# One queue for the first loads, a mixed priority for the planner, and state stores on the scalar engine's queue, in an eight-core diffusion step

## The chip, the cores and the metric

The kernel runs on all eight cores of one Trainium2 chip. Each core runs the same program on its own data. The time is the device time of the slowest core in microseconds (us); lower is better. The profile is that of one execution, taken on the slowest core.

## The reference, cut to what matters

Two trunk layers of width 1024 are applied to 512 context tokens (two new requests of 256) and 1024 latent tokens per core.

```
h = rmsnorm(x) * (1 + sc) + sh                      # sc, sh, g: six slices of silu(c) @ ada_w
layer 0:  q, k, v, g, lr_f, lr_b, fin = split(h @ ev_w_in)
          o  = gated linear attention, both directions, 4 heads, scan over chunks:
               S = decay * S + k^T v ;  o = q S + masked(q k^T) v
          o  = rmsnorm(o) * silu(g) ;  fo = Re(2-D DFT(fin))
          x += g_m * (concat(o, fo) @ ev_w_out)
layer 1:  gelu / spatial gating and a gated width-3 convolution, then an output projection
both:     x += g_f * (relu(h @ ffn_w1)^2 @ ffn_w2)
out:      rmsnorm(x), and the final scan states of the context requests (fwd and bwd)
```

## The kernel before, in words

The 1536 tokens of a core lie in three chunks of 512: chunks m = 0 and 1 are latent, m = 2 is context. `xT[m]` (2 MB, float32) holds the residual, `hT[m]` the normalised bfloat16 input. Weights come in units of 1 MB in bfloat16, cast from 2 MB of float32 on the way by the GpSimd queue, into six slots (`NW = 6`). The slot of each unit is fixed by program order (`wload`), so a unit can be loaded only when the unit six places before it in its slot has been read for the last time. Two units, `qk0` and `qk1`, hold their slots for longer (`pinned`).

The program records operations in program order (`R.add`, one `seq` number each). A planner (`schedule`) then gives each engine a fixed order: step by step it takes, over all engines, the operation that can start earliest by its own cost figures, and where several can start at the same time, the one with the lowest `prio`. Before the change `prio` is `seq`. The engines then run their lists in order, with semaphore waits where one depends on another. The planner charges a switch of the scalar engine's function table 1300 ns, and it gives out the eight banks of PSUM.

In program order the work is: four units of the adaLN projection (`ada0_s0` to `ada0_s3`), each needed by two of the eight columns of the first norm; the norm of chunks 0 and 1; `evc` (the small input projections, weight `evC`: decay inputs `lrT` and Fourier input `finT`); `xcs_tile`; the norm and `evc` of chunk 2; then for head 0 `Dunit` (decays, four activations of 1024 columns) and `QK`; the values and gates `vg` of 12 token tiles by three units; `headS(h)` for the latent tokens of the four heads, with eight scan steps (`step`) in a chain and four output pairs (`opair`); `headP(h)` for the context tokens, two steps each, whose final states are stored to `ns`; the DFTs; `og_T`, the output projection `outproj`; the norm; and the FFN, in which each unit of `wf1` is used for twelve groups (four output columns times three chunks) and each of `wf2` for six.

During the attention the space of `xT` holds other tiles (`vtokS`, `sprevS`, `xcs`, `qke`), so x is loaded a second time before the output projection: chunks 0 and 1 when those tiles are free, chunk 2 after the last context head. `Rp` holds the context scan states and is used again by each head, so the first state copy of head h + 1 waits until the stores of head h have landed.

All first loads of x and the stores go through the SyncE queue (SP); all cast loads through the GpSimd queue (POOL).

Of the kernel before, what the change touches and what calls it, by code (L numbers as in the profile page):

```python
# [7 lines left out]
BF16 = mybir.dt.bfloat16  # L8
# [30 lines left out]

class Op:  # L40
    __slots__ = ("eng", "parts", "seq", "prio", "tab", "lat", "dma", "newpt", "pts",
                 "succ", "npred", "ext", "ready", "start", "fin", "key", "val", "dur")


class Rec:
# [105 lines left out]
    def schedule(self):  # L151
        ops = self.ops
# [3 lines left out]
        for o in ops:  # L156
            preds = set()
            for _, deps, _ in o.parts:
                preds |= deps
            o.npred = len(preds)  # L160
            for p in preds:
                p.succ.append(o)
        cand = {e: [] for e in self.ENGS}
        for o in ops:
            if o.npred == 0:
# [169 lines left out]
def _consts():  # L335
    c = {}
    s = np.arange(128)[:, None]
    t = np.arange(128)[None, :]
    cb = np.zeros((128, 1152), np.float32)
    cb[:, 0:128] = np.eye(128)  # L340
    cb[:, 128:256] = (s <= t) / 16.0
    cb[:, 256:384] = (s >= t) / 16.0
    cb[:, 384:512] = (s <= t)
    cb[:, 512:640] = (s >= t)
    a = np.arange(64)
    ang = 2 * np.pi * ((a[:, None] * a[None, :]) % 64) / 64.0
    for g in range(2):
        cb[g * 64:(g + 1) * 64, 640 + g * 64:640 + (g + 1) * 64] = np.cos(ang)
        cb[g * 64:(g + 1) * 64, 768 + g * 64:768 + (g + 1) * 64] = np.sin(ang)
    cb[:, 896:1024] = 1.0 / 1024  # L350
    cb[:, 1024:1152] = 1.0
    c["cb"] = cb
    mats = {}
    for L in (256, 1024):
        tt = np.arange(L, dtype=np.int64)
        ang = 2 * np.pi * ((tt[:, None] * tt[None, :]) % L).astype(np.float64) / L
        sc = 1.0 / np.sqrt(64.0 * L)
        mats[L] = ((np.cos(ang) * sc).astype(np.float32), (-np.sin(ang) * sc).astype(np.float32))
    u = [mats[1024][k][:, m * 512:(m + 1) * 512].reshape(8, 128, 512).transpose(1, 0, 2)
         for m in range(2) for k in range(2)]  # L360
    c["dft1024"] = np.ascontiguousarray(np.stack(u).reshape(4, 128, 4096))
    u = [mats[256][k].reshape(2, 128, 256).transpose(1, 0, 2) for k in range(2)]
    c["dft256"] = np.ascontiguousarray(np.stack(u, 2).reshape(128, 1024))
    return c
# [5 lines left out]
def build():  # L370
    nc = bass.Bass("TRN2", target_bir_lowering=False)

    def din(name, shape):
        return nc.dram_tensor(name, list(shape), F32, kind="ExternalInput").ap()
# [15 lines left out]
    wodo_d = din("wodo", [2, 128, 4096])  # L390
    wf1_d = din("wf1", [16, 128, 4096])
    wf2_d = din("wf2", [16, 128, 4096])
    cb_d = din("cb", [128, 1152])
    dft1024_d = din("dft1024", [4, 128, 4096])
    dft256_d = din("dft256", [128, 1024])
    y_d = dout("y", [3, 8, 128, 512])
# [2 lines left out]
    with contextlib.ExitStack() as es:  # L399
        A0 = (nc.sbuf_base + 63) // 64 * 64  # L400
        R = Rec(nc, es)
        cur = [A0]

        def at(nbytes):
            a = cur[0]
            cur[0] += (nbytes + 63) // 64 * 64
            assert cur[0] <= nc.sbuf_usable_end, cur[0]
            return a


        cb = R.sb("cb", [128, 1152], BF16, at(2304))
        identb, tri = cb[:, 0:128], [cb[:, 128:256], cb[:, 256:384]]
        mask2, cs64, onesb = cb[:, 384:640], cb[:, 640:896], cb[:, 896:1024]
        ones33 = cb[0:33, 1024:1152]
        wsT = R.sb("wsT", [128, 512], BF16, at(1024))
        w2aug = R.sb("w2aug", [64, 1024], BF16, at(2048))
        gbr = R.sb("gbr", [33, 512], BF16, at(1024))
        pp = R.sb("pp", [128, PP_N], F32, at(PP_N * 4))
        scT = R.sb("scT", [128, 8, 2], BF16, at(32))
        cst = R.sb("cst", [128, 2], F32, at(8))  # L420
        modT = [R.sb("modT%d" % l, [128, 48, 2], F32, at(384)) for l in range(2)]
        gsc = [R.sb("gsc%d" % l, [128, 2, 8, 2], F32, at(128)) for l in range(2)]
# [60 lines left out]
            R.add(q, [(lambda: h.dma_start(out=dst, in_=src), [], 1000 if q == "pool" else 100)], W=[dst],  # L483
                  dma=(key, nbytes), prio=prio)

        def store(dst, src, key, nbytes):
            R.add("sp", [(lambda: nc.sync.dma_start(out=dst, in_=src), [src], 100)], W=[], dma=(key, nbytes))


        wpos = [0]  # L490
# [13 lines left out]
        def w8(name, src, pin=None):  # L504
            return wload(name, src, 4096, pin)[:].rearrange("p (k n) -> p k n", k=8)
# [4 lines left out]
        def cload(dst, src, q):  # L510
            ksp[0] += 1
            load(q, dst, src, "dc%d" % ksp[0], nfree(dst) * 128 * 4)

        R.add("dve", [(lambda: nc.vector.memset(cst[:, 0:1], EPS), [], 70)], W=[cst[:]])
        R.add("dve", [(lambda: nc.vector.memset(cst[:, 1:2], 1.0), [], 70)], W=[cst[:]])
        cload(pp[:], pp_d, "sp")
        load("sp", xT[0][:].rearrange("p c t -> p (c t)"), x_d[0], "dx0", 2 << 20)
        act(scT[:], pp[:, PP_COND:PP_COND + 16].rearrange("p (c k) -> p c k", k=2), AF.Silu, [pp[:]], [scT[:]], tab="silu")

        def evac_mod(l, ps, c0, nch, pc0):  # L520
# [35 lines left out]
        def norm_stats(m, x):  # L556
            ps = PT(R)
            parts = []
            for c in range(8):
                sq = ring(sqr)  # L560
                act(sq[:], x[:, c, :], AF.Square, [x[:, c, :]], [sq[:]])
                R.add("pe", [(lambda sq=sq, c=c: nc.tensor.matmul(ps.f(), onesb, sq[:], start=(c == 0), stop=(c == 7)), [sq[:], onesb], 216)], W=[ps])  # L562
            r = ring(rsr)
            act(r[:], lambda: ps.f(), AF.Ln, [ps, cst[:]], [r[:]], tab="nle", bias=cst[:, 0:1])
            act(r[:], r[:], AF.Exp, [r[:]], [r[:]], tab="nle", scale=-0.5)
            return r
# [27 lines left out]

        for u in range(4):
            ada_unit("ada0_s%d" % u, wada_d[u], 0, [(u * 2, 2, 0), (8 + u * 2, 2, 2)])
            if u == 0:
                cload(cb[:], cb_d, "pool")
        norm(0, 0, 0)
        load("sp", xT[1][:].rearrange("p c t -> p (c t)"), x_d[1], "dx1", 2 << 20)  # L600
        norm(0, 0, 1)
        load("sp", xT[2][:].rearrange("p c t -> p (c t)"), x_d[2], "dx2", 2 << 20)


        xo = [a_x]
# [34 lines left out]
        vtok = lambda j: vtokS[:, j, :] if j < 8 else vtokP[:, j - 8, :]  # L640
        sprev = lambda d, j: sprevS[:, d, j, :] if j < 8 else sprevP[:, d, j - 8, :]

        cload(w2aug[:], w2aug_d, "pool")
        R.add("pool", [(lambda: nc.gpsimd.memset(lrT[32:64, :], 0.0), [], 900)], W=[lrT[:]])
        R.add("pool", [(lambda: nc.gpsimd.memset(lrT[32:33, :], 1.0), [], 900)], W=[lrT[:]])

        wc = wload("evC", wevc_d, 2304)[:].rearrange("p (k n) -> p k n", k=8)

        def evc(m):
            p = PT(R)  # L650
# [87 lines left out]
        def step(h, fw, i, Rt, d_is, seqn):  # L738
# [20 lines left out]
            for d in range(2):  # L759
# [10 lines left out]
                if last:  # L770
                    j = tl[d]
                    act(r[:], r[:], AF.Identity, [r[:], dc[:]], [r[:]], scale=dc[:, d, j:j + 1])
                    store(ns_d[d, seqn, h], r[:], "dns%d%d" % (d, seqn), 128 * 768)

        def opair(h, ja):

# [63 lines left out]
            for d in range(2):  # L840
                load("sp", Rs[h % 2][d][:], s0_d[d, h], "ds0%d%d" % (h % 2, d), 128 * 768)

        wqk = {0: w8("qk0", wev_d[0], 0)}
        wv = [w8("vg%d" % u, wev_d[2 + u]) for u in range(3)]
        wqk[1] = w8("qk1", wev_d[1], 1)
        norm(0, 0, 2)
        evc(2)
# [46 lines left out]
        ada(0, 2)  # L894
        wO = [w8("evO%d" % i, wevo_d[i]) for i in range(2)]
        for m in range(2):
            load("sp", xT[m][:].rearrange("p c t -> p (c t)"), x_d[m], "dx%d" % m, 2 << 20)

        def outproj(l, wo, src, m):
            for oc in range(8):  # L900
# [14 lines left out]
        norm(0, 1, 0)  # L915
        for j in range(8, 12):
            og_T(j)
        load("sp", xT[2][:].rearrange("p c t -> p (c t)"), x_d[2], "dx2", 2 << 20)
        outproj(0, wO, hT, 2)
        norm(0, 1, 1)  # L920
        norm(0, 1, 2)
# [253 lines left out]
```

How the kernel before makes its waits and increments, by code:

```python
    def emit(self):  # L269
# [31 lines left out]
                    if need.get(d.key, 0) < d.val:  # L301
                        need[d.key] = d.val
                items = sorted(need.items(), key=lambda kv: kv[0])
                semof = lambda key: sem[key] if key in sem else self.dsem[key]
                todo = []
                for key, val in items:
                    if know[e].get(key, 0) < val:
                        todo.append((key, val))
                        learn(e, key, val)
                for key, val in todo[:-1]:
                    H[e].wait_ge(semof(key), val)
                ins = fn()
                if todo:
                    ins._wait_ge(semof(todo[-1][0]), todo[-1][1])
# [4 lines left out]
                dcnt[key] = dcnt.get(key, 0) + 16  # L319
                ins.then_inc(self.dsem[key], 16)
                o.key, o.val = key, dcnt[key]
            else:
                cnt[e] += 1
                ins.then_inc(sem[e], 1)
                o.key, o.val = e, cnt[e]
            snap[(o.key, o.val)] = dict(know[e])
        for key, val in list(dcnt.items()):
            if know["sp"].get(key, 0) < val:
                nc.sync.wait_ge(self.dsem[key], val)
        for e in self.ENGS:
            if cnt[e] and know["sp"].get(e, 0) < cnt[e]:
                nc.sync.wait_ge(sem[e], cnt[e])
```

## Time and profile before

| what | value |
|---|---|
| time, median of 3 runs | 1254.83 us (1253.84 to 1268.19) |
| the profiled execution's own time | 1252.24 us |
| its span on the slowest core | 1250.9 us (all cores 1237.9 to 1250.9) |
| TensorE (PE) busy | 1138.3 us, 91% |
| VectorE (DVE) busy | 451.0 us, 36% |
| ScalarE (ACT) busy | 437.5 us, 35% |
| read from HBM | 171.5 MB |

The span is the time from the first to the last instruction; 1.3 us of the execution lie outside it. PE is the busiest engine by far, and the other engines matter where PE waits for them.

### The profile page before, as it was taken

To read this page: it belongs to the slowest core of one execution; us is meant where nothing else is said; L and a number is where in the kernel's file an instruction comes from. 1 tells how busy PE (TensorE), PEld (TensorE's weight loads), DVE (VectorE), ACT (ScalarE), POOL (GpSimd) and SP (SyncE) were. 2 spreads that over 40 slices of the span, in tenths; PEclk is the share of its full clock that TensorE was granted. 3 is DMA by queue.
4 is the path that set the end of the run, shared out by engine and by line. 5 is a ranking of instruction groups with operands and counts; after the bars stand their busy time and mean duration, and the time that the engine had idled before them with its cause. 6 is when DMAs were issued, how large, how long until landed. Compare 5 with 4: busy or idle time off the path is not lost.

```text
span 1250.9 us, 15212 instructions; the slowest of 8 cores (1237.9 to 1250.9 us)
## 1 busy us (share of the span) xinstructions
PE 1138.3 (91%) x6288; PEld 542.5 (43%) x6288; DVE 451.0 (36%) x883; ACT 437.5 (35%) x834; POOL 48.4 (4%) x109
## 2 busy tenths in 40 slices
PE   0599978789849999999999999999999999999995
PEld 0144455454414444444444444444444444444442
DVE  0364156676633222222222341456532222222226
ACT  1661377753644320023310383225543100332013
POOL 2000000000000000000000000000000000000000
PEclk9699989889969999999999989999999999999997
DMA  9984241569783245447535212105313131310005
GB/s 236 175 140 74 42 89 26 85 118 223 119 181 68 37 98 101 80 90 135 100 58 112 45 25 39 30 1 101 68 35 68 34 68 34 68 34 1 1 1 201
DMA packets 19344, 101.36 MB, mean 81 GB/s; under 512 B 2155, under 2 KB 5483, under 8 KB 9036
## 3 DMA queue, kind: packets, MB, share of 16 engines
q0 software_dynamic: 11312, 79.01, 35.5%
q1 hardware_dynamic: 7964, 21.39, 5.2%
q8 instruction: 49, 0.80, 0.3%
q14 instruction: 19, 0.16, 0.0%
HBM read 171.53 MB, written 7.86 MB: 143 GB/s over the span
## 4 chain that ended last, share of the span: by engine, by line
PE 81%; DMA 10%; ACT 4%; DVE 3%; issue 1%; POOL 0%; DVEq 0%; ACTq 0%; POOLq 0%
PE ps L461 79%; DMA w_ada_s_77<-wada 4%; DMA xT_73<-x 3%; DMA ns<-RP_93 2%; PE ps L1007 1%; PE ps L562 1%; DMA w_ada_3_0_129<-wada 1%; ACT sprevS L471 1%; ACT hT_68 L471 0%; ACT hT_69 L471 0%; ACT sq_59 L471 0%; ACT junk L471 0%; DVE og L799 0%; ACT t_3_101 L471 0%; ACT sq_60 L471 0%
## 5 line engine op out<-in xcount | busy, mean ns | idle before, releaser
L471 ACT ACTIVATE relu_65<-ps 128x512 bf16<-128x512 f32 x64 | 38.2, 597 | 242.0 <-PE ps L461 242.0
L471 ACT ACTIVATE relu_67<-ps 128x512 bf16<-128x512 f32 x64 | 38.2, 597 | 68.2 <-PE ps L461 68.2
L471 ACT ACTIVATE relu_66<-ps 128x512 bf16<-128x512 f32 x64 | 38.2, 597 | 67.1 <-PE ps L461 67.1
L938 DVE TENSOR_TENSOR aT_133<-relu_65 128x512 bf16<-128x512 bf16 x60 | 25.5, 426 | 79.0 <-ACT relu_65 L471 79.0
L938 DVE TENSOR_TENSOR aT_135<-relu_67 128x512 bf16<-128x512 bf16 x60 | 25.5, 426 | 78.1 <-ACT relu_67 L471 78.1
L938 DVE TENSOR_TENSOR aT_134<-relu_66 128x512 bf16<-128x512 bf16 x60 | 25.5, 426 | 75.9 <-ACT relu_66 L471 75.9
L471 ACT ACTIVATE sq_58<-xT_71 128x512 bf16<-128x512 f32 x15 | 9.4, 628 | 113.1 <-PE ps L562 87.5
L582 DVE SCALAR_TENSOR_TENSOR xT_73<-ps,modT_50,xT_73 128x512 f32<-128x512 f32 x24 | 17.4, 748 | 53.6 <-PE ps L461 41.4
L582 DVE SCALAR_TENSOR_TENSOR xT_73<-ps,modT_51,xT_73 128x512 f32<-128x512 f32 x24 | 18.0, 751 | 50.9 <-PE ps L461 50.9
L582 DVE SCALAR_TENSOR_TENSOR xT_72<-ps,modT_50,xT_72 128x512 f32<-128x512 f32 x24 | 17.9, 750 | 50.1 <-PE ps L461 46.7
L582 DVE SCALAR_TENSOR_TENSOR xT_71<-ps,modT_51,xT_71 128x512 f32<-128x512 f32 x24 | 18.0, 751 | 48.7 <-PE ps L461 48.7
L582 DVE SCALAR_TENSOR_TENSOR xT_71<-ps,modT_50,xT_71 128x512 f32<-128x512 f32 x24 | 17.7, 750 | 48.9 <-PE ps L461 47.8
L582 DVE SCALAR_TENSOR_TENSOR xT_72<-ps,modT_51,xT_72 128x512 f32<-128x512 f32 x24 | 17.7, 750 | 47.0 <-PE ps L461 47.0
L562 PE MATMUL ps<-sq_58,cb 128*128 128x512 bf16 x40 | 17.3, 434 | 11.1 <-DMA cb<-cb 7.9
L471 ACT ACTIVATE og<-ps 128x256 bf16<-128x256 f32 (+1 forms) x24 | 11.8, 491 | 43.3 <-DVE vtokS L592 24.7
L471 ACT ACTIVATE junk<-ps 128x192 bf16<-128x192 f32 x48 | 15.8, 329 | 22.0 <-PE ps L461 21.7
L562 PE MATMUL ps<-sq_59,cb 128*128 128x512 bf16 x40 | 17.7, 443 | 4.2 <-ACT sq_59 L471 3.6
L461 PE MATMUL ps<-scT,w_ada_s_74 128*128 128x2 bf16 x32 | 1.0, 166 | 22.2 <-DMA w_ada_s_74<-wada 22.2
L562 PE MATMUL ps<-sq_60,cb 128*128 128x512 bf16 x40 | 17.6, 440 | 4.0 <-ACT sq_60 L471 3.4
L471 ACT ACTIVATE sq_60<-xT_71 128x512 bf16<-128x512 f32 x10 | 6.3, 626 | 42.1 <-DVE xT_71 L582 36.0
L523 DVE TENSOR_TENSOR modT_50<-ps,pp 128x4 f32<-128x4 f32 (+1 forms) x16 | 2.2, 158 | 51.0 <-PE ps L461 51.0
L799 DVE SCALAR_TENSOR_TENSOR og<-ps,rs,og 128x192 bf16<-128x192 f32 x48 | 17.7, 410 | 6.4 <-ACT rs L471 6.1
(719 smaller groups left out, 2412.8 us busy)
## 6 DMA issues: line engine op xcount, KB each, us to landing
xT_71<-x SPq DMA_DIRECT2D x2, 2048.0 KB, 16.2
xT_72<-x SPq DMA_DIRECT2D x2, 2048.0 KB, 27.2
xT_73<-x SPq DMA_DIRECT2D x2, 2048.0 KB, 35.9
w_ada_s_74<-wada POOLq DMA_DIRECT2D x1, 1024.0 KB, 20.6
w_ada_s_75<-wada POOLq DMA_DIRECT2D x1, 1024.0 KB, 37.1
w_ada_s_76<-wada POOLq DMA_DIRECT2D x1, 1024.0 KB, 43.1
w_ada_s_77<-wada POOLq DMA_DIRECT2D x1, 1024.0 KB, 49.9
w_qk_115<-wev POOLq DMA_DIRECT2D x1, 1024.0 KB, 56.1
```

Source lines behind the costliest of these rows:

```text
L461: parts.append((lambda view=view, l=l, r=r, i=i, n=n: nc.tensor.matmul(view(), l, r, start=(i == 0), stop=(i == n - 1)), [l, r], max(27.0, ...
L471: R.add("act", [(lambda: nc.scalar.activation(out=o(), in_=i(), func=func, **kw), Rd, dur)], W=W, tab=tab)
L523: lambda: nc.vector.tensor_tensor(out=modT[l][:, c0:c0 + nch, :], in0=ps.f(pc0 * 2, (pc0 + nch) * 2).rearrange("p (c k) -> p c k", k=2), i ...
L562: R.add("pe", [(lambda sq=sq, c=c: nc.tensor.matmul(ps.f(), onesb, sq[:], start=(c == 0), stop=(c == 7)), [sq[:], onesb], 216)], W=[ps])
L582: lambda: nc.vector.scalar_tensor_tensor(out=x[:, oc, :], in0=ps.f(), scalar=modT[l][:, gch + oc, CI(m):CI(m) + 1], in1=x[:, oc, :], op0=A ...
L799: lambda o_=o_, t=t: nc.vector.scalar_tensor_tensor(out=o_, in0=ps.f(t * 192, t * 192 + 192), scalar=rs[:, k + t:k + t + 1], in1=o_, op0=A ...
L938: vop(2, [a], [rl[:]], lambda a=a, rl=rl: nc.vector.tensor_tensor(out=a, in0=rl[:], in1=rl[:], op=ALU.mult))
L1007: parts.append((lambda g=g, l_=l_, r_=r_, i=i, p=p: nc.tensor.matmul(p.f(g * 128, (g + 1) * 128), l_, r_, start=(i == 0), stop=(i == 1)), ...
```

## The change

The planner's priority becomes 30 times the sequence number minus `bl`, the longest path in the planner's nanoseconds from the operation to the end of the program (a DMA counts with its issue and a fixed latency in it, not with its transfer). The first loads of x move from the SP queue to the POOL queue, where they stand in one list with the weights; the second loads stay on SP. `w2aug`, `cb`, `evC`, `qk0` and `vg0` are recorded earlier, before or between the first norms. The matrix of 1/1024 that the norm's sums use is no longer part of `cb`; VectorE sets it by a memset. The stores of the context states go to the scalar engine's queue; the stores of y stay on SP.

```
+        for o in reversed(ops):
+            o.bl = o.dur + o.lat + max([x.bl for x in o.succ], default=0)
+        for o in ops:
+            o.prio = 30.0 * o.seq - o.bl
...
-    cb = np.zeros((128, 1152), np.float32)
+    cb = np.zeros((128, 1024), np.float32)
...
-    cb[:, 896:1024] = 1.0 / 1024
-    cb[:, 1024:1152] = 1.0
+    cb[:, 896:1024] = 1.0
...
+        onesb = R.sb("ones", [128, 128], BF16, at(256))
...
-        def store(dst, src, key, nbytes):
-            R.add("sp", [(lambda: nc.sync.dma_start(out=dst, in_=src), [src], 100)], W=[], dma=(key, nbytes))
+        def store(dst, src, key, nbytes, q="sp"):
+            h = nc.scalar if q == "act" else nc.sync
+            R.add(q, [(lambda: h.dma_start(out=dst, in_=src), [src], 100)], W=[], dma=(key, nbytes))
...
+        R.add("dve", [(lambda: nc.vector.memset(onesb[:], 1.0 / 1024), [], 130)], W=[onesb[:]])
         cload(pp[:], pp_d, "sp")
-        load("sp", xT[0][:].rearrange("p c t -> p (c t)"), x_d[0], "dx0", 2 << 20)
+        xload = lambda m, q: load(q, xT[m][:].rearrange("p c t -> p (c t)"), x_d[m], "dx%d%s" % (m, q), 2 << 20)
+        xload(0, "pool")
...
         for u in range(4):
             ada_unit("ada0_s%d" % u, wada_d[u], 0, [(u * 2, 2, 0), (8 + u * 2, 2, 2)])
-            if u == 0:
-                cload(cb[:], cb_d, "pool")
+        cload(w2aug[:], w2aug_d, "pool")
+        cload(cb[:], cb_d, "pool")
+        wc = wload("evC", wevc_d, 2304)[:].rearrange("p (k n) -> p k n", k=8)
+        wqk = {0: w8("qk0", wev_d[0], 0)}
         norm(0, 0, 0)
-        load("sp", xT[1][:].rearrange("p c t -> p (c t)"), x_d[1], "dx1", 2 << 20)
+        xload(1, "pool")
         norm(0, 0, 1)
-        load("sp", xT[2][:].rearrange("p c t -> p (c t)"), x_d[2], "dx2", 2 << 20)
+        wv = [w8("vg0", wev_d[2])]
+        xload(2, "pool")
...
-                    store(ns_d[d, seqn, h], r[:], "dns%d%d" % (d, seqn), 128 * 768)
+                    store(ns_d[d, seqn, h], r[:], "dns%d%d" % (d, seqn), 128 * 768, "act")
...
-        wqk = {0: w8("qk0", wev_d[0], 0)}
-        wv = [w8("vg%d" % u, wev_d[2 + u]) for u in range(3)]
+        wv += [w8("vg%d" % u, wev_d[2 + u]) for u in (1, 2)]
...
-            load("sp", xT[m][:].rearrange("p c t -> p (c t)"), x_d[m], "dx%d" % m, 2 << 20)
+            xload(m, "sp")
```

## Rows read from the trace of the kernel before

**Rows 1.** The page: PE's busy tenths in 40 slices of the span.

```profile
PE   0599978789849999999999999999999999999995
```

**Rows 2.** Busy time by stretch: us of the stretch, then PE, PEld, DVE, ACT, POOL, PEclk, DMA.

```profile
58.50:152.00 93.50, 93.48 (x463) 43.14 (x463) 36.94 (x62) 40.04 (x67) 2.41 (x8) 0.98 0.52 90
152.00:278.00 126.00, 100.28 (x870) 65.03 (x868) 83.24 (x221) 89.68 (x230) 7.86 (x28) 0.89 0.41 75
278.00:310.00 32.00, 30.05 (x203) 15.71 (x201) 20.29 (x44) 10.18 (x28) 1.37 (x4) 0.96 0.94 228
...
328.00:372.00 44.00, 23.75 (x137) 9.78 (x135) 20.72 (x31) 22.55 (x40) 1.58 (x3) 0.78 0.93 175
372.00:700.00 328.00, 328.00 (x1859) 153.84 (x1858) 80.68 (x165) 68.39 (x115) 13.71 (x26) 1.00 0.45 85
...
58.50:372.00 313.50, 263.81 (x1846) 143.41 (x1846) 173.07 (x390) 171.81 (x395) 14.80 (x45) 0.91 0.58 110
```

**Rows 3.** The chain that ended last, in order of time: start us, us, what.

```profile
153.25 0.81 ACT sprevS L471 x2
...
277.81 28.15 DMA ns<-RP_93
...
327.88 37.48 DMA xT_73<-x
```

**Rows 4.** The timeline of PE: start us, us, instruction, idle before and releaser.

```profile
53.67 1.01 PE L461 MATMUL ps<-scT,w_ada_s_77 128*128 128x2 bf16 x32 [6.26 <-DMA w_ada_s_77<-wada]
...
58.47 1.89 PE L461 MATMUL ps<-hT_68,w_evC 128*32 128x512 bf16 x4
...
366.28 0.99 PE L461 MATMUL ps<-scT,w_ada_0_0_141 128*128 128x2 bf16 x32 [16.34 <-DVE xT_73 L582]
```

**Rows 5.** DMA issues of 0 to 80 us: count, KB written, us from issue to landing.

```profile
xT_73<-x SPq DMA_DIRECT2D x1, 2048.0 KB, 34.4
...
w_evC<-wevc POOLq DMA_DIRECT2D x1, 576.0 KB, 51.7
cb<-cb POOLq DMA_DIRECT2D x1, 288.0 KB, 28.8
w2aug<-w2aug POOLq DMA_DIRECT2D x1, 128.0 KB, 50.0
```

**Rows 6.** The page, DMA queues: packets, MB written, packet time as share of 16 engines.

```profile
q0 software_dynamic: 11312, 79.01, 35.5%
q1 hardware_dynamic: 7964, 21.39, 5.2%
```

**Rows 7.** What PE waited for from 152 to 278 us: us in total, times, longest.

```profile
PE ps L461 <- ACT sprevS L471: 7.3, 3, 4.6
PE ps L461 <- DMA w_ada_3_0_129<-wada: 3.9, 1, 3.9
PE ps L461 <- ACT junk L471: 3.4, 9, 0.7
PE ps L461 <- DVE ket_104 L735: 2.8, 1, 2.8
```

**Rows 8.** The timeline of the DMA issues on SP.

```profile
272.40 0.34 SPq L483 DMA_DIRECT2D xT_71<-x  x1
```

**Rows 9.** The timeline of POOL, the first unit of the FFN.

```profile
341.73 0.53 POOL L483 DMA_DIRECT2D w_f_0_0_136<-wf  x1 [17.79 <-PE ps L461]
```

**Rows 10.** DMA issues of 250 to 345 us, columns as in rows 5.

```profile
w_f_0_0_136<-wf POOLq DMA_DIRECT2D x1, 1024.0 KB, 17.9
ns<-RP_93 SPq DMA_DIRECT2D x4, 96.0 KB, 9.5
```

**Rows 11.** DMA issues of the whole span, a weight unit and a store of y.

```profile
w_ada_0_1_142<-wada POOLq DMA_DIRECT2D x1, 1024.0 KB, 8.2
...
y<-ys_191 SPq DMA_DIRECT2D x4, 256.0 KB, 2.5
```

**Rows 12.** ACT's groups of instructions over the whole span: its table loads.

```profile
L471 ACT ACT_TABLE_LOAD x8 | 10.3, 1283 | 1.2 <-PEq L371 1.1
```

More of the change, by code:

```diff
@@ L41 @@
     __slots__ = ("eng", "parts", "seq", "prio", "tab", "lat", "dma", "newpt", "pts",
-                 "succ", "npred", "ext", "ready", "start", "fin", "key", "val", "dur")
+                 "succ", "npred", "bl", "ext", "ready", "start", "fin", "key", "val", "dur")
 class Rec:
@@ L392, in build @@
     wf2_d = din("wf2", [16, 128, 4096])
-    cb_d = din("cb", [128, 1152])
+    cb_d = din("cb", [128, 1024])
     dft1024_d = din("dft1024", [4, 128, 4096])
@@ L408, in at @@
             return a
-        cb = R.sb("cb", [128, 1152], BF16, at(2304))
+        cb = R.sb("cb", [128, 1024], BF16, at(2048))
         identb, tri = cb[:, 0:128], [cb[:, 128:256], cb[:, 256:384]]
-        mask2, cs64, onesb = cb[:, 384:640], cb[:, 640:896], cb[:, 896:1024]
-        ones33 = cb[0:33, 1024:1152]
+        mask2, cs64 = cb[:, 384:640], cb[:, 640:896]
+        ones33 = cb[0:33, 896:1024]
         wsT = R.sb("wsT", [128, 512], BF16, at(1024))
@@ L561, in norm_stats @@
                 act(sq[:], x[:, c, :], AF.Square, [x[:, c, :]], [sq[:]])
-                R.add("pe", [(lambda sq=sq, c=c: nc.tensor.matmul(ps.f(), onesb, sq[:], start=(c == 0), stop=(c == 7)), [sq[:], onesb], 216)], W=[ps])
+                R.add("pe", [(lambda sq=sq, c=c: nc.tensor.matmul(ps.f(), onesb[:], sq[:], start=(c == 0), stop=(c == 7)), [sq[:], onesb[:]], 216)], W=[ps])
             r = ring(rsr)
@@ L641, in build @@
         sprev = lambda d, j: sprevS[:, d, j, :] if j < 8 else sprevP[:, d, j - 8, :]
-        cload(w2aug[:], w2aug_d, "pool")
         R.add("pool", [(lambda: nc.gpsimd.memset(lrT[32:64, :], 0.0), [], 900)], W=[lrT[:]])
         R.add("pool", [(lambda: nc.gpsimd.memset(lrT[32:33, :], 1.0), [], 900)], W=[lrT[:]])
-        wc = wload("evC", wevc_d, 2304)[:].rearrange("p (k n) -> p k n", k=8)
         def evc(m):
@@ L917, in build @@
             og_T(j)
-        load("sp", xT[2][:].rearrange("p c t -> p (c t)"), x_d[2], "dx2", 2 << 20)
+        xload(2, "sp")
         outproj(0, wO, hT, 2)
```

## The prediction

> **What bounds the kernel now.** Read the page first: PE is busy 9 tenths or more in most of the 40 slices of 31 us, and falls short in the first two, in slices 6 to 12 (all but the tenth) and at the end [rows 1]. So PE sets the time, and the change can win only where PE is idle. The busy time by stretch says where [rows 2]: from 58.5 to 152 us PE is full, from 152 to 278 it is idle for 126.00 - 100.28 = 25.7 us, from 328 to 372 for 44.00 - 23.75 = 20.3 us, and from 372 to 700, in the FFN, not at all. Between 58.5 and 372 the idle sum is 313.5 - 263.8 = 49.7 us. Then the chain of work that ended last names the culprits [rows 3]: head 0's chain of steps, which begins at 153 us, 28 us of a state store, 37 us of the second load of x for chunk 2. The timeline of PE shows the last of the first weight units awaited until 53.67, the first dense matmul at 58.47, and a wait of 16.34 us at 366.28 for the residual of chunk 2 [rows 4].
>
> The sum is made against the profiled execution, 1252.2 us, 2.6 us (0.2%) under the median of the runs shown.
>
> **The first loads.** Before, x0, x1 and x2 go out on SP at once and share the 16 engines with the weights. I order the new single list by hand with the planner's own figures. In us and relative to the path of head 0's first state update, 30 times the sequence number minus the path gives: x0 -29.0, ada0_s0 -24.5, s1 -22.8, s2 -21.12, x1 -21.09, s3 -19.4, evC -12.1, w2aug -9.4, x2 -7.4, then cb and qk0, both -6.2. x2 drops behind evC; the two near ties change little.
>
> Price: before, all these bytes but qk0 were there when evC landed, at 6.2 + 51.7 = 57.9 us [rows 5]. A cast load reads twice the KB that it writes, so three x and four ada units are 7 x 2.1 MB, evC 1.18, cb 0.59 and w2aug 0.26, together 16.7 MB in 56.4 us from the first issue at 1.5 us, or 3.38 us per MB. In the new order six of the seven big loads end with s3: 12.6 MB x 3.38 + 1.5 = 44.1 us; evC at 48.1. From s3's landing to the first evC matmul it took 58.47 - 53.67 = 4.8 us [rows 4]; so PE starts at 48.9, 9.6 us earlier. What is late next: the two first chunks of evc are 48 matmuls, 10.4 us at the planner's 0.216 and more at the lower clock, to about 61; x2 lands at 56.2, cb at 57.9, no later than evC did, and qk0 at 65, no earlier than before, because the same bytes stand ahead of it. The short Fourier and decay matmuls fill part of that. I let 2.6 us be lost and take a gain of **7 us**.
>
> No row shows an uncast load on the software queue. From below its price is that of the hardware queue, 5.2% of 1251 us for 21.39 MB = 3.0 us per MB; from above the software queue's per MB written, 35.5% for 79.01 MB = 5.6 [rows 6], which makes x 11.8 us instead of the 7.1 in my sum. I take the 3.38 of the mixed stretch, since a plain copy reads what it writes, as on the hardware queue. At the upper end x0 and x1 cost 2 x 4.7 = 9.4 us more and the term is about -2. So -2 to 9.6. The memset and the shorter cb cost nothing on the path: DVE is idle then, and the norm's sums no longer wait for cb, a wait that lies before the ada units land anyway.
>
> **The planner's order.** The `prio` only decides between operations that can start at the same time, so it acts where PE has a choice, in the dense 58.5 to 152 us. There the sequence put all 36 vg tiles and part of the DFTs ahead of head 0's steps. By the new figure a head is 129 operations (3.9 us) and some 7.0 us of path after the one before: the first steps of the four heads stand at 8.9, 19.8, 30.7 and 41.6 (us, minus the same path), a vg tile of the second unit at about 18, of the third at about 35. So heads 0 to 2 start beside the vg work, as soon as vg0 is there (some 72 us), some 75 us earlier than before, and the 40 us of later vg tiles become what PE does while the chain of steps waits for ACT and DVE. These two are busy only 89.7 and 83.2 of 126 us there [rows 2]; they are no bound.
>
> How much of the 25.7 us comes back? The waits of 1 us and more are those that a matmul group of 1.7 us fills: sprevS 7.3, the ada unit 3.9, ket_104 2.8, together **14 us** [rows 7]. The rest are waits under 1 us, such as junk with 9 for 3.4 us, shorter than the error of a plan made ahead; I leave them. The granted clock is 0.89 in this stretch and 0.98 in the full one before it [rows 2]; full speed would make 100.3 us into 91 at best. I take **3** of these 0 to 9.
>
> **The stores and the second load of x.** At 272.40 SP issues x0 and x1 again [rows 8]; the state store of 277.81 stands behind these 4 MB in the same queue and takes 28.15 us [rows 3], against a median of 9.5 for such a store and 2.5 for one of y [rows 10, 11]. The next context head waits for it. On ACT's queue nothing stands ahead: 19 to 26 us come off the chain of context heads. PE loses nothing there now, 30.05 of 32 us are covered by the output projection [rows 2]; what is won is that the last context head, and with it the second load of x2, comes some 20 us earlier while that projection is still to do. Then the 16.34 us wait goes. Late next is the FFN's first unit, whose slot is free only when the projection of chunk 2 is done: issued at 341.73, landed 17.9 later, at 359.6 [rows 9, 10]. PE ended at 366.28 - 16.34 = 349.9, so 9.7 us would stay and 6.6 be won; if that load has the engines to itself it takes some 8.2 us, as a later ada unit did [rows 11], and all 16 are won. Between 6.6 and 16.3 I take **12**; 0 if the store is no faster.
>
> The Trainium skill speaks against this part: "DMA: Bandwidth & Descriptors", section "Issuing engines are not separate DMA queues", holds that DMAs of all issuing engines interleave on the same 16 engines, and that another issuing engine only saves sequencer time. By that rule this term is 0 and the sum 1232. The same page, "Queues, rings and completion order", gives SP and ACT a row of rings each, with the engines taking turns between rows, and by that the term stands.
>
> **What it costs.** The gates of vg use another ACT table than the decays. Before there are 8 table loads of 1.28 us [rows 12]; interleaving may add 0 to 24 (one there and one back for each of 12 tiles), 0 to 31 us of ACT time. ACT has room; I take six more, 7.7 us, and **2 us** of it on PE's path. 16 store issues on ACT at about the 0.34 us of an issue on SP [rows 8] are 5.4 us, each behind its own scaling and ahead of the next head's decays: **1 us** on the path, 0 to 5. In the FFN the priority prefers chunk 0 of several units over chunks 1 and 2 of the first (their norms follow one another in the path, about 6 us apart, and a unit is only 1.1 to 1.3 us of sequence): **1 us**, 0 to 42 (below). The end, the last norm and its stores, has no choice: 0.
>
> Sum: 7 + 14 + 3 + 12 - 2 - 1 - 1 = 32 us; 1252.2 - 32 = **1220**.
>
> **The rivals.** (a) The order hardly changes: the earliest start decides before any priority, and the gates' banks and tables keep the heads behind the vg work. Then 7 us of the start and 5 of the stores remain: 1240. For it: PE alone has the choice. Against: PE is full from 58.5 to 152, which is just where it has one.
> (b) PE never waits between its start and the FFN: 48.9 + 263.8 = 312.7 instead of 372, 59 us, 1193. For it: ACT and DVE are 55% busy in that stretch [rows 2]. Against: the short waits, and the slot of the FFN's first unit.
> (c) The stores win nothing, because x0 and x1 fill the engines (DMA share 0.94 [rows 2]) whatever the queue: 1220 + 12 = 1232. Against: the store's 9.5 us median has fewer bytes ahead of it, not fewer engines. It is what the page's first rule would make.
> (d) Slower: in the FFN, chunk 0 runs ahead over the units, so a unit's slot comes free only after its chunk 2, late and in bunches, and PE meets its units as they land. A unit gives 6.9 us of one chunk (32 matmuls at the planner's 0.216) against 8.2 of a landing [rows 11]; 1.3 us for each of 32 units is 42 us, and 1262. That is the other 32 us gone and 10 more; beyond 1.0 us per unit the kernel is slower than before, beyond 1.9 us (1280) by over 2%. For it: PE is at 328.00 of 328 now, so nothing can be won there and anything lost shows. Against: DMA share 0.45 [rows 2], and chunks 1 and 2 are always there to do.
>
> **How the numbers follow.** Forecast 0.54 (own range 1204 to 1236), (a) 0.13, (b) 0.13, (c) 0.10, (d) 0.10. The range 1190 to 1248 leaves out (d) and the faster half of (b), with the tails. About 2% is what a measurement of this kernel tells from no change, so 1230 and 1280 are the bounds. Faster by over 2%: four fifths of the forecast, all of (b), two fifths of (c): 0.60. Slower: half of (d), 0.05. Within: 0.35.
>
> **What would show it.** In the profile after: x2 landing behind evC on the software queue and the first evC matmul near 49 us; sprevS of head 0 near 80 us and not 153 [rows 3], among vg matmuls; PE's idle time between 150 and the FFN at about half; state stores landing in 3 to 10 us, no 16 us wait for xT_73; the FFN's first matmul near 335 and not 372. Wrong would be: a DMA wait of PE at each FFN unit (d), head 0 still after the last vg tile (a), or an x load of 12 us on the software queue.

## The result and the profile after

The changed kernel takes 1224.66 us in the median (1220.13 to 1237.79) against 1254.42: the ratio is 0.9752, with a 95% interval of 0.9717 to 0.9787. That is 2.5% faster; 1220 was predicted. In some executions of either kernel, 1237.79 here, one die ran at a lower granted clock than the other, and the ratios, here and below, leave these out. The profiled execution took 1223.98 us.

The page of the changed kernel: its span, PE's busy tenths, and ACT's table loads (before: [rows 1, 12]).

```profile
span 1222.9 us, 15139 instructions; the slowest of 8 cores (1206.9 to 1222.9 us)
...
PE   1599998839899999999999999999999999999995
...
L475 ACT ACT_TABLE_LOAD x16 | 20.5, 1283 | 1.3 <-PEq L374 1.1
```

The busy time by stretch, columns as in [rows 2].

```profile
49.10:75.00 25.90, 24.27 (x124) 10.69 (x125) 14.97 (x23) 21.27 (x32) 0.31 (x2) 0.89 1.02 199
75.00:145.00 70.00, 69.90 (x423) 35.70 (x421) 39.82 (x91) 39.79 (x83) 1.98 (x8) 1.00 0.32 57
145.00:225.00 80.00, 71.82 (x547) 41.60 (x544) 45.44 (x123) 63.92 (x142) 5.24 (x17) 1.00 0.46 72
225.00:285.00 60.00, 37.15 (x327) 22.78 (x328) 31.18 (x78) 21.97 (x72) 3.57 (x11) 0.83 0.88 183
...
350.40:693.00 342.60, 342.60 (x1873) 159.61 (x1871) 88.63 (x173) 80.44 (x134) 13.19 (x25) 1.00 0.45 82
...
49.10:350.40 301.30, 262.29 (x1849) 141.23 (x1850) 173.19 (x391) 183.99 (x409) 14.80 (x45) 0.93 0.62 118
```

The chain that ended last, in order of time, answers to [rows 3].

```profile
4.81 44.27 DMA w_evC<-wevc
49.12 7.01 PE ps L465 x24
...
229.13 36.57 DMA ns<-RP_99
```

The timeline of PE, for [rows 4]: the first and the eighth vg tile, head 0's first state matmul, and the longest wait.

```profile
77.77 1.89 PE L465 MATMUL ps<-w_vg_81,hT_69 128*128 128x512 bf16 x8
...
89.85 1.89 PE L465 MATMUL ps<-w_vg_81,hT_70 128*128 128x512 bf16 x8
...
99.59 0.33 PE L465 MATMUL ps<-vtokS,ket_108 128*128 128x192 bf16 x2
...
266.14 0.40 PE L465 MATMUL ps<-qke_86 128*128 128x128 bf16 x2 [17.73 <-DVE RP_99 L769]
```

The first dense matmul comes 9.4 us earlier, head 0's steps 53 us earlier and beside the vg tiles, and the wait for xT_73 is gone. In its place the slowest core waits 17.7 us for a state copy behind a state store that landed only after 36.6 us. Between the first dense matmul and the FFN PE is idle for 301.3 - 262.3 = 39.0 us, where it was 49.7. The list of the cores shows that this core is not the rule.

```profile
core 4: 1222.9 us, clock 0.961
...
die 0 (median of its cores): 1211.1 us, clock 0.972
die 1 (median of its cores): 1211.8 us, clock 0.977
```

So the median core gained 1244.2 - 1211.8 = 32 us and the slowest 28, and the time is that of the slowest. A table of first matmuls, each the median over the eight cores of the profiled execution, read from the timelines of PE, carries the rest (us; the rows from the third on are the experiments; "head 0's step" is its first state matmul, "last step" the last state matmul of a latent head, "proj. 2" the first matmul of the output projection of chunk 2 that reads the Fourier tile `foP`, some 2 us behind the first of all).

| kernel | evC | head 0's step | last step | proj. 2 | FFN | span, median core | slowest core |
|---|---|---|---|---|---|---|---|
| before | 57.8 | 151.8 | 252.2 | 336.6 | 365.5 | 1244.2 | 1250.9 |
| changed | 48.7 | 98.0 | 225.4 | 320.4 | 338.0 | 1211.8 | 1222.9 |
| loads only | 45.2 | 158.6 | 261.4 | 348.4 | 377.0 | 1256.8 | 1264.2 |
| priority only | 57.6 | 98.7 | 230.9 | 326.0 | 343.4 | 1216.2 | 1220.8 |
| stores only | 58.4 | 152.9 | 254.4 | 340.8 | 365.4 | 1244.0 | 1244.4 |
| changed, stores on SP | 48.8 | 98.8 | 225.9 | 329.4 | 347.3 | 1221.1 | 1222.9 |
| priority and ACT stores | 58.0 | 98.4 | 231.2 | 327.4 | 344.6 | 1218.4 | 1220.2 |
| changed, two Rp | 49.4 | 99.1 | 226.0 | 314.7 | 340.3 | 1219.2 | 1225.0 |
| priority, ACT stores, two Rp | 57.7 | 98.7 | 231.3 | 313.3 | 345.1 | 1223.0 | 1230.2 |
| priority in the attention only | 58.3 | 99.1 | 231.5 | 327.0 | 344.4 | 1222.5 | 1226.4 |
| changed, slot | 48.1 | 97.8 | 224.7 | 316.9 | 330.5 | 1213.8 | 1216.7 |
| changed, two Rp, slot | 48.0 | 97.9 | 224.1 | 313.5 | 335.2 | 1221.8 | 1226.1 |
| priority, ACT stores, slot | 56.6 | 97.7 | 229.8 | 318.3 | 331.3 | 1215.2 | 1219.9 |
| path alone | 56.4 | 96.6 | 231.3 | 331.4 | 350.6 | 1232.4 | 1240.2 |

### The profile page after: what moved, and what is told of

Its sections match the earlier page's. It is cut to its first block, busy times and chain, and to the rows that moved or that the text cites. A ratio compares the mean times of both kernels' runs of the same rounds, so it can differ in the third digit from the quotient of the medians.

```text
span 1222.9 us, 15139 instructions; the slowest of 8 cores (1206.9 to 1222.9 us)
## 1 busy us (share of the span) xinstructions
PE 1131.7 (93%) x6288; PEld 539.3 (44%) x6288; DVE 449.0 (37%) x884; ACT 447.3 (37%) x842; POOL 50.0 (4%) x112
## 4 chain that ended last, share of the span: by engine, by line
PE 86%; DMA 7%; ACT 3%; DVE 3%; issue 1%; POOL 0%; ACTq 0%; DVEq 0%; POOLq 0%
PE ps L465 83%; DMA w_evC<-wevc 4%; DMA ns<-RP_99 3%; PE ps L569 1%; PE ps L1013 1%; ACT hT_70 L475 1%; ACT sq_61 L475 0%; DVE hT_71 L816 0%; ACT sprevS L475 0%; ACT hT_69 L475 0%; DVE hT_70 L816 0%; ACT sp_107 L475 0%; ACT sq_60 L475 0%; PE ps L811 0%; DVE RS_94 L775 0%
## 5 line engine op out<-in xcount | busy, mean ns | idle before, releaser
L589 DVE SCALAR_TENSOR_TENSOR xT_72<-ps,modT_51,xT_72 128x512 f32<-128x512 f32 x24 | 18.0, 751 | 47.8 <-PE ps L465 47.6
L569 PE MATMUL ps<-sq_59,ones 128*128 128x512 bf16 x40 | 16.7, 418 | 15.5 <-ACT sq_59 L475 15.1
L475 ACT ACTIVATE sq_59<-xT_72 128x512 bf16<-128x512 f32 x15 | 9.4, 627 | 51.9 <-PE ps L569 22.3
L569 PE MATMUL ps<-sq_61,ones 128*128 128x512 bf16 x40 | 16.8, 420 | 8.7 <-ACT sq_61 L475 8.1
L475 ACT ACTIVATE sq_61<-xT_73 128x512 bf16<-128x512 f32 x15 | 9.4, 624 | 33.3 <-PE ps L569 25.6
L465 PE MATMUL ps<-qke_86 128*128 128x128 bf16 x24 | 3.4, 235 | 19.2 <-DVE RP_99 L769 17.7
L569 PE MATMUL ps<-sq_60,ones 128*128 128x512 bf16 x40 | 16.6, 414 | 2.0 <-ACT sq_60 L475 1.5
## 6 DMA issues: line engine op xcount, KB each, us to landing
xT_72<-x POOLq DMA_DIRECT2D x1, 2048.0 KB, 11.4
xT_74<-x POOLq DMA_DIRECT2D x1, 2048.0 KB, 48.4
xT_74<-x SPq DMA_DIRECT2D x1, 2048.0 KB, 15.8
```

Source lines behind the costliest of these rows:

```text
L465: parts.append((lambda view=view, l=l, r=r, i=i, n=n: nc.tensor.matmul(view(), l, r, start=(i == 0), stop=(i == n - 1)), [l, r], max(27.0, ...
L475: R.add("act", [(lambda: nc.scalar.activation(out=o(), in_=i(), func=func, **kw), Rd, dur)], W=W, tab=tab)
L589: lambda: nc.vector.scalar_tensor_tensor(out=x[:, oc, :], in0=ps.f(), scalar=modT[l][:, gch + oc, CI(m):CI(m) + 1], in1=x[:, oc, :], op0=A ...
```

## The experiments

Each group of four ran on one chip with its own runs of the kernel before (medians 1257.3, 1259.2 and 1253.4 us), so ratios are compared and not times. The same holds for the table: in these runs the median core of the kernel before takes 1247.3 us beside the first group (loads only, priority only, stores only, changed with stores on SP), 1247.0 beside the second (priority and ACT stores, changed with two Rp, both together, attention only) and 1244.0 beside the third (the rows with "slot" and the path alone), and 1244.2 in the table. Of a difference between rows of different groups some 3 us can be the chip's.

**One part at a time.** The three parts of the change, each alone on the kernel before, and the changed kernel with the third undone.

Loads only: the changed kernel without

```
-            o.prio = 30.0 * o.seq - o.bl
...
-                    store(ns_d[d, seqn, h], r[:], "dns%d%d" % (d, seqn), 128 * 768, "act")
+                    store(ns_d[d, seqn, h], r[:], "dns%d%d" % (d, seqn), 128 * 768)
```

> The kernel before with the first loads in one queue in program order and the memset, but with the old priority and the state stores on SP. Theory (the prediction's first term): the first dense matmul comes some 9 us earlier and 7 us of it stay, 1247 us against 1254. Rival: the same bytes stand ahead of qk0 and vg0, so the earlier start is eaten before 75 us and the time is 1254. With the old priority the list on the queue is x0, the four ada units, w2aug, cb, evC, qk0, x1, x2, so chunk 1 comes later than in the changed kernel; a second rival is that this costs more than the early start gives, 1258.

Measured: 1265.5 us, ratio 1.0058 (1.0037 to 1.0079), 0.6% slower. The second rival holds, at twice its price: 8 us over the kernel before of its group, where it said 4. evC comes 12.6 us earlier, but in program order x1 and x2 stand behind qk0. DMA issues from 7 to 12 us, and PE's waits from 45 to 80 us:

```profile
xT<-x POOLq DMA_DIRECT2D x2, 2048.0 KB, 55.5
```

```profile
PE ps L565 <- ACT sq L471: 8.8, 3, 4.0
PE ps L461 <- DMA w_evC<-wevc: 3.3, 1, 3.3
```

PE waits for the squares of chunk 1, and head 0's first step is 6.8 us later than before.

Priority only: the kernel before with

```
+        for o in reversed(ops):
+            o.bl = o.dur + o.lat + max([x.bl for x in o.succ], default=0)
+        for o in ops:
+            o.prio = 30.0 * o.seq - o.bl
```

> The kernel before with the new priority alone; loads and stores as before. Theory: 14 + 3 us of the idle time of the attention come back and 2 to 4 are lost, 1241 us. Rival (b) of the prediction, the order is nearly everything: 1228. Rival (a), the order hardly acts: 1252.

Measured: 1222.4 us, ratio 0.9719 (0.9700 to 0.9737): the gain of the whole change, and 35 us. That is beyond rival (b)'s 1228 as the expectation put it. Its busy time by stretch, on its slowest core:

```profile
75.00:145.00 70.00, 68.77 (x428) 36.84 (x435) 40.87 (x92) 46.02 (x89) 2.08 (x11) 1.00 0.23 41
145.00:225.00 80.00, 74.36 (x493) 42.58 (x500) 42.52 (x105) 60.38 (x127) 4.94 (x15) 0.96 0.53 82
225.00:285.00 60.00, 51.30 (x440) 31.61 (x446) 37.33 (x98) 28.60 (x88) 4.09 (x12) 0.83 0.88 180
```

PE is idle for 5.6 us of the 80 after 145 and for 8.7 of the next 60, and no wait for the residual of chunk 2 is left among the eleven longest. The FFN begins 22 us earlier on the median core (table), and 6 more are won after that. In its own group the median core gains 1247.3 - 1216.5 = 31 us and the slowest 35.

What the 28 us of the table consist of can be read from the traces of the two kernels, again as medians over the cores. From the first evC matmul to the first FFN matmul PE's idle time falls from 42.0 to 25.2 us, and 15 of these 17 us lie before the last latent step (23.8 to 8.9). The same matmuls also take 5 us less there, at a granted clock of 0.95 and not 0.92. Core 0 of the kernel before and core 5 of this one, each from its first evC to its first FFN matmul:

```profile
58.14:364.21 306.07, 266.42 (x1845) 143.70 (x1845) 172.53 (x389) 171.39 (x396) 14.81 (x45) 0.92 0.58 111
56.98:342.67 285.69, 259.51 (x1845) 141.45 (x1845) 171.87 (x390) 184.94 (x408) 14.80 (x45) 0.95 0.62 116
```

Behind the FFN's first matmul 2 us of idle time go, and the matmuls take 4 us less.

Stores only: the kernel before with the stores of the states on ACT's queue.

```
+            h = nc.scalar if q == "act" else nc.sync
...
-                    store(ns_d[d, seqn, h], r[:], "dns%d%d" % (d, seqn), 128 * 768)
+                    store(ns_d[d, seqn, h], r[:], "dns%d%d" % (d, seqn), 128 * 768, "act")
```

> The kernel before with only the state stores moved to the scalar engine's queue. Theory: the store no longer stands behind x0 and x1, lands in 3 to 10 us, the last context head and the second load of x2 come some 20 us earlier, and the wait for xT_73 goes: 1242 us. Rival (c): the engines are full whatever the queue, the stores land no sooner and the time is 1254.

Measured: 1247.7 us, ratio 0.9913 (0.9893 to 0.9932). The time falls by 11 us, close to the theory's 12, and part of its way is seen. The wait for x2, 16.3 us on the slowest core in [rows 4] and 5.7 to 8.5 us on the other seven, is 4.0 us on each of the eight cores. On the slowest:

```profile
PE ps L461 <- DVE xT L583: 4.0, 1, 4.0
```

So the wait shrinks by 12 us on the slowest core and by some 4 on the others. The times move alike: over the runs of the group the slowest core gains 1256.0 - 1245.5 = 10.5 us and the median core 1247.3 - 1243.6 = 3.7. The stores themselves do not land in 3 to 10 us: the four behind x0 and x1 take 17.8 to 28.9 us over the eight cores, where they took 26.1 to 28.7, and those of the last context head 11.4 to 38.7, where they took 10.3 to 28.0. What is gained at one head is lost at another.

The changed kernel with the stores back on SP:

```
-                    store(ns_d[d, seqn, h], r[:], "dns%d%d" % (d, seqn), 128 * 768, "act")
+                    store(ns_d[d, seqn, h], r[:], "dns%d%d" % (d, seqn), 128 * 768)
```

> The changed kernel with the state stores back on SP. Theory: the store behind x0 and x1 lands 10 to 20 us later again and the time goes up by up to 12 us, to 1236. Rival (c): nothing is lost, 1224. A second rival: on SP the stores stand ahead of x0 and x1 when they are issued before them, and the long landing of 36.6 us seen beside x0 and x1 goes: 1215.

Measured: 1225.0 us, ratio 0.9741 (0.9723 to 0.9760), no different from the change. But the cores differ:

```profile
die 0 (median of its cores): 1221.1 us, clock 0.973
die 1 (median of its cores): 1219.6 us, clock 0.967
```

The median core is 9 us slower than in the changed kernel, 6 to 7 with the chips' difference taken off, and the slowest, 1222.9, is the same. ACT's queue won this on most cores and lost it on the slowest, which is another one in each execution of the changed kernel: core 4 in the profiled one, core 0 and core 1 in two more.

**Is it the store's landing, and are the loads worth anything?** Two sets of state tiles let a context head start without waiting for the stores of the last one. The second set lies in the space of the FFN's `relu` tiles, which nothing uses during the attention.

```
+        rl0 = cur[0]
         rlr = [R.sb("relu%d" % i, [128, 512], BF16, at(1024)) for i in range(3)]
...
+        a_q = rl0
+        Rq = [[R.sb("RQ%d%d" % (s, d), [128, 192], F32, a_q + (s * 2 + d) * 768) for d in range(2)] for s in range(2)]
...
-                    store(ns_d[d, seqn, h], r[:], "dns%d%d" % (d, seqn), 128 * 768, "act")
+                    store(ns_d[d, seqn, h], r[:], "dns%d%d%d" % (h % 2, d, seqn), 128 * 768, "act")
...
-                    step(h, fw, i, Rp[s], None, s)
+                    step(h, fw, i, (Rq if h % 2 else Rp)[s], None, s)
```

> The changed kernel with two sets of Rp, used by even and odd context heads, so that a head's first state copy waits for the stores of the head before the last and no longer for the last. Theory: on the slowest core of the changed kernel PE waits 17.7 us for a state copy behind a store that landed 36.6 us after its issue, while the median core is 11 us faster; without that wait the slowest core comes near the median core, 1213 us against 1224. Rival: the second loads of x and the slot of the first FFN unit end no earlier, 1222.

Measured: 1224.5 us, ratio 0.9734 (0.9711 to 0.9757). The 1213 us of my theory were not reached; the time is near the rival's. The wait for the state copy is gone, under 1 us on each of the eight cores, and the projection of chunk 2 comes 6 us earlier, but the FFN 2 us later (table, two chips). What PE waits for from 200 to 350 us, on the slowest core:

```profile
PE ps L466 <- DMA w_ada<-wada: 6.2, 1, 6.2
PE ps L466 <- DVE xT L590: 3.6, 1, 3.6
...
PE ps L466 <- DMA w_f<-wf: 2.1, 1, 2.1
```

Three other transfers of the same stretch took the store's place: an adaLN unit, x2 and the first FFN unit.

The second set also has a price of its own, which I had overlooked: it holds the space of `relu` until the last head's stores have landed, and on each of the eight cores the first `relu` of the FFN waits for them. ACT and PE on the slowest core:

```profile
361.04 4.85 ACT L476 ACTIVATE relu<-ps 128x512 bf16<-128x512 f32 x9 [12.93 <-DMA ns<-RQ]
...
361.69 4.49 PE L466 MATMUL ps<-hT,w_f 128*128 128x512 bf16 x20 [2.89 <-ACT relu L476]
```

PE loses 0 to 5.4 us to it, 3 in the median, and nothing in the changed kernel. So this run and the two below with two sets do not show what the landing alone is worth; a second set in a space of its own was not tried.

The change without its first part:

```
-        xload(0, "pool")
+        load("sp", xT[0][:].rearrange("p c t -> p (c t)"), x_d[0], "dx0", 2 << 20)
...
-        xload(1, "pool")
+        load("sp", xT[1][:].rearrange("p c t -> p (c t)"), x_d[1], "dx1", 2 << 20)
```

and so on: the order of recording and `cb` are those of before.

> The changed kernel without its first part: priority and state stores on ACT's queue, but the first loads as before. Theory after the first runs: the first loads in one queue are worth nothing beside the priority, since head 0's first state update comes at 98 us with them and without them; 1218 to 1224 us, no slower than the changed kernel. Rival (the prediction's term): they are worth 7 us and this is 1231.

Measured: 1222.0 us, ratio 0.9712 (0.9692 to 0.9733): no slower than the change. The prediction's term fell as far as the time goes. On the median core the loads did win, 1218.4 against 1211.8 in the changed kernel, some 4 of it beyond the chips' difference; but there the slowest core lies 7, 11 and 13 us over the median in three executions, and here only 2 to 4 (1218.4 and 1220.2 in the profiled one). With the stores on SP the two kernels with and without the loads ran on one chip (table: "changed, stores on SP" and "priority only"): the last step comes at 225.9 against 230.9, so 5 us of the early start last that long, but from there PE is idle for 21.9 us until the FFN against 16.6, and the FFN comes 4 us later.

Both together on the kernel before, two sets and no new loads:

```
+            o.prio = 30.0 * o.seq - o.bl
...
+                    step(h, fw, i, (Rq if h % 2 else Rp)[s], None, s)
...
+                    store(ns_d[d, seqn, h], r[:], "dns%d%d%d" % (h % 2, d, seqn), 128 * 768, "act")
```

> The kernel before with the priority, the stores on ACT's queue and two sets of Rp. Theory: 1210 to 1214 us, as the changed kernel with two sets, or a little less. Rival: the loads in one queue matter here, when the context heads no longer wait, and this is 7 us over the changed kernel with two sets.

Measured: 1231.2 us, ratio 0.9777 (0.9754 to 0.9801), 0.65% slower than with one set. The theory fell: the projection of chunk 2 begins 14 us earlier and the FFN no earlier. On the slowest core PE waits 8.7 us for the first FFN unit and 4.7 for the first `relu`.

The priority for the attention alone:

```
...
+            o.prio = 30.0 * o.seq - (o.bl if o.seq < self.cut else 0.0)
...
+        R.cut = len(R.ops)
         for m in ffn(0, hooks0):
```

> The kernel before with the new priority only for the operations recorded before the FFN of layer 0; from there on the sequence number alone. Theory: the attention gives 22 us (first FFN matmul at 343 us and not 365), and the 5 us after it are the priority's too and go: 1228 us against 1222 with the priority everywhere. Rival (d) of the prediction: in the FFN the priority holds slots and costs something, so that this is faster, 1218.

Measured: 1226.8 us, ratio 0.9758 (0.9734 to 0.9782), against 0.9719 (0.9700 to 0.9737) with the priority everywhere; they ran in different groups. The theory holds within that: the FFN begins at 344.4 as with the priority everywhere (343.4), and from there to the end the median core takes 1222.5 - 344.4 = 878 us, as before the change (1244.2 - 365.5 = 879), where the full priority takes 1216.2 - 343.4 = 873; on the same chip, with priority and ACT stores, it takes 1218.4 - 344.6 = 874. Most of the difference are waits for the squares of the later norms. PE on the slowest core from 343 us to the end, with the priority in the attention only and everywhere:

```profile
PE ps L566 <- ACT sq L475: 6.6, 9, 1.4
PE ps L566 <- ACT sq L475: 2.7, 5, 1.0
```

**What is late next, and the sequence term.** The first FFN unit goes two slots further on in the ring, to one that an adaLN unit leaves early:

```
+        wpos[0] += 2
         for m in ffn(0, hooks0):
```

> The changed kernel with the first FFN unit two slots further on in the ring, in the slot that an adaLN unit frees early and no longer in that of the output projection's first unit. Theory: with one set of Rp the FFN's first matmul follows the projection of chunk 2 with some 2 us of PE idle before it on the median core, so the slot is covered and nothing changes, 1222 to 1225 us. Rival: the planner uses the earlier unit to begin the FFN with chunk 0 while the context heads still wait, 1212.

Measured: 1218.8 us, ratio 0.9727 (0.9709 to 0.9744). The FFN begins 7.5 us earlier, against the theory; but the median span is 1213.8, where the changed kernel has 1211.8, so the time is given back behind it. The traces show where: from the FFN's first matmul to the first of layer 1 each core of the changed kernel takes 345.0 us with PE full, and here 354.2 to 355.0. That stretch, on core 7 of the changed kernel and of this one, and what PE waits for in it here:

```profile
338.04:683.04 345.00, 345.00 (x1940) 161.62 (x1939) 89.63 (x176) 82.27 (x138) 14.25 (x27) 1.00 0.48 82
331.67:685.88 354.21, 351.28 (x1979) 163.54 (x1978) 92.91 (x182) 86.28 (x144) 15.31 (x29) 0.99 0.55 85
```

```profile
PE ps L465 <- ACT hT L475: 2.8, 5, 1.7
```

So the FFN begins before its inputs are all there. Of the 9 to 10 us 3 are idle, in which PE waits for `hT`, the norm's output; 3 are small matmuls of the norm and of adaLN that stood ahead of the FFN before (39 more in the line); and some 4 are slower matmuls. Behind the stretch both take the same, 528 us. The ratio is 0.25% under the change's, with intervals that overlap: no difference shown.

With two sets of Rp as well:

```
+                    step(h, fw, i, (Rq if h % 2 else Rp)[s], None, s)
...
+        wpos[0] += 2
```

> The changed kernel with two sets of Rp and the first FFN unit in an earlier slot. With two sets alone the projection of chunk 2 came 6 us earlier and the FFN no earlier. Theory: it was the slot of the FFN's first unit that was late next; with both the FFN begins 8 us earlier and the time is 1215 us. Rival: the second load of x for chunk 2 or PE's own work is late next and this is 1224.

Measured: 1227.1 us, ratio 0.9790 (0.9775 to 0.9806). The FFN begins 5 us earlier than with two sets alone and the kernel is slower: the theory holds for the slot and fails for the time. On the slowest core PE then waits 6.5 us for an adaLN unit and 1.6 for the first `relu`.

And without the new loads:

```
+            o.prio = 30.0 * o.seq - o.bl
...
+                    store(ns_d[d, seqn, h], r[:], "dns%d%d" % (d, seqn), 128 * 768, "act")
...
+        wpos[0] += 2
```

> The kernel before with the priority, the stores on ACT's queue and the first FFN unit in an earlier slot; first loads as before. Theory: as without the slot, 1220 us, since one set of Rp holds the context heads. Rival: 1212, the planner begins the FFN beside the context heads.

Measured: 1221.2 us, ratio 0.9738 (0.9720 to 0.9756). The FFN begins 13 us earlier than without the slot, and no gain is left at the end: the stretch to layer 1 takes 355 us again, where it takes 345 without the slot.

The path alone as priority, shown against the kernel with the priority only:

```
-            o.prio = 30.0 * o.seq - o.bl
+            o.prio = -o.bl
```

> The kernel before with the longest path alone as priority, without the sequence term. Theory: the sequence term is a tie breaker in the attention, where the paths of the heads lie 7 us apart, and matters in the FFN, where without it a chunk runs ahead over all units that are there: rival (d) of the prediction in its pure form, PE waits at units of the FFN and the time is 1240 us or more. Rival: chunks 1 and 2 cover the loads all the same, and it is as good as the mixed priority, 1222.

Measured: 1247.4 us, ratio 0.9946 (0.9926 to 0.9967). The sequence term is worth 2.3% of the time (0.9719 against 0.9946). The time is the theory's, the mechanism isn't. A stretch of the FFN by busy time, and PE's waits over the span, on the slowest core:

```profile
345.00:690.00 345.00, 344.19 (x1901) 160.08 (x1900) 91.17 (x178) 81.34 (x136) 14.25 (x27) 1.00 0.46 83
```

```profile
PE ps L465 <- DVE RP L766: 12.3, 2, 9.5
PE ps L465 <- ACT sprevP L475: 8.1, 1, 8.1
```

PE doesn't wait for units of the FFN. On the median core 7 us are lost before the FFN, where PE waits in the context heads, and 1232.4 - 350.6 = 882 us lie behind its beginning, 9 more than with the mixed priority. Up to layer 1 the two take the same (344 and 345 us); the 9 lie in layer 1 and the second FFN. Why was not tried.

## Why the prediction was right, and where it was not

The total was right, 1220 for 1224.7, and its place: the attention. Three of its terms were not: where it had 7, 14 + 3 and 12 us, the runs show nothing for the first and the third beside the second, and 35 for the second alone. Their errors cancelled; that the sum came out near the time is luck.

- **The order and landing of the first loads** were right. The issues on POOL and the landings of the DMAs of 0 to 80 us in the changed kernel:

```profile
5.33 0.60 POOL L487 DMA_DIRECT2D w2aug<-w2aug  x1
7.29 0.56 POOL L487 DMA_DIRECT2D xT_74<-x  x1
20.76 0.53 POOL L487 DMA_DIRECT2D w_vg_81<-wev  x1 [10.01 <-PE ps L465]
```

```profile
xT_74<-x POOLq DMA_DIRECT2D x1, 2048.0 KB, 48.4
...
w_vg_81<-wev POOLq DMA_DIRECT2D x1, 1024.0 KB, 50.9
...
w_evC<-wevc POOLq DMA_DIRECT2D x1, 576.0 KB, 44.3
w2aug<-w2aug POOLq DMA_DIRECT2D x1, 128.0 KB, 44.5
```

  evC was issued at 4.81 and landed at 49.1 (48.1 forecast); the list of issues is the one computed. What failed is the worth, "7 us": the step that failed is "I let 2.6 us be lost". Head 0's first state matmul comes at 98.0 us with the new loads and at 98.7 with the priority alone. It waits for the two QK groups and eight vg tiles, 69.9 to 91.6 us, and vg0 landed at 20.76 + 50.9 = 71.7, where it landed at 23.54 + 47.8 = 71.3 before:

```profile
23.54 0.53 POOL L483 DMA_DIRECT2D w_vg_116<-wev  x1 [14.40 <-PE ps L461]
...
w_vg_116<-wev POOLq DMA_DIRECT2D x1, 1024.0 KB, 47.8
```

  The 9 us at the front were filled with other work. For some 5 us of it this is work that the head chain no longer holds (127.5 us from first to last step against 132.5), so the last step does come earlier; but this was lost again, before the FFN with the stores on SP, and on the slowest core with the stores on ACT. Alone the part costs 0.6%; beside the priority with stores on SP the ratio is 0.9741 against 0.9719, with stores on ACT 0.9752 against 0.9712. No run shows a gain in the time.
- **The steps as filler** were right in kind: head 0's steps beside the vg tiles, full PE from 75 to 145 us. "As soon as vg0 is there (some 72 us)" was too early, since I left out those eight tiles and QK, 22 us. The idle time was priced well, 15 us for 14 on the median core, and faster matmuls brought 5 for 3. Not in the sum at all are 6 us behind the FFN's beginning, where I had put -1, and that the slowest core comes nearer to the median one (35 us against 31). PE's idle time from 150 us to the FFN was to fall to about half; in the changed kernel it falls from 42.0 to 26.3 us on the median core and from 49.7 to 37.3 on the slowest.
- **The stores**, 12 us, were the third, and what failed is the adding: this term and the priority remove the same wait. The wait for x2, which I gave to the stores, goes with the priority alone on each core, because the context heads come some 20 us earlier with everything else (first state store at 232 and not 253 us). So the part gives 11 us alone, and beside the priority nothing: 0.9741 and 0.9752, 0.9719 and 0.9712. The landing was wrong too. A store on ACT's queue did not land in 3 to 10 us. The four from each tile of `Rp` had medians of 7.7 to 17.5 us over the eight cores, before 7.4 to 15.8, and the one on the slowest core's path took 36.6. Beside the priority that is rival (c), and the rule of the Trainium skill behind it ("DMA: Bandwidth & Descriptors", "Issuing engines are not separate DMA queues"): the trace agrees for these medians, with a DMA share of 0.88 in that stretch. The store's own landing, from 228.5 to 235 us:

```profile
ns<-RP_100 ACTq DMA_DIRECT2D x1, 96.0 KB, 24.0
ns<-RP_99 ACTq DMA_DIRECT2D x1, 96.0 KB, 36.6
```

- **The costs**: table loads went from 8 to 16 (14 forecast, six more), 10 us of ACT. Rival (d) did not occur: PE is at 342.60 of 342.6 us in the FFN.
- **What is late next**, the slot of the FFN's first unit, was right: freed, it brings the FFN 5 to 13 us forward. That this is given back by the first matmul of layer 1 was not foreseen: an FFN that begins before its inputs are all there waits inside.

So -0.6, 2.8 and 0.9% alone don't add up to the 2.5% together: the parts are not independent. Two of them remove one wait, and each one also changes the whole list that the planner writes.

## What to carry to other kernels

Where a greedy planner orders in-order engines, the priority among ready operations can be worth more than any wait that a profile names: a long chain with idle partners should start beside the dense work, not behind it, with program order kept as a second term. An earlier first matmul was worth nothing in the time here, since the long chain's first operation had another last input; look for that one. Before adding two terms, ask whether one change removes the wait that the other was priced by. Before pricing a wait in a profile of the slowest core, look at the same wait on the other cores, and compare cores on one chip: here the same kernel's median core differed by 3 us between chips. Space that is idle when an experiment borrows it is not free if a transfer still reads it when its owner comes back.

## What the runs showed of the hardware

The uncast load of x on the software queue was no dearer than the 3.0 us per MB that the prediction had for the hardware queue: x2 landed at 7.29 + 48.4 = 55.7 us, right behind w2aug at 5.33 + 44.5 = 49.8, 5.9 us for 2.1 MB or 2.8 us per MB. Stores of 96 KB on ACT's queue landed within 3.5 us at a DMA share of 0.41 (slowest core, 276 to 281 us) and after 36.6 us beside 4 MB of x and four weight units, at a share of 0.97 to 1.02, on the same core in the same execution; on core 6 the same store took 7.5 us.

The stretch from the FFN's first matmul to layer 1 took 345.0 us on each of the eight cores of the changed kernel, with PE full at a granted clock of 1.00 (2.4 GHz) on core 7.
